# Two transformer blocks on one core: the attention pipeline's slots in another order, and one stream of groups in the second block

## The chip, the cores and the metric

The kernel runs on one core of a Trainium2 chip. The time is what the device needs for one execution of the whole program, in microseconds (us). All weights and activations are float32, and every matrix product goes through TensorE (PE), which also does the transposes. VectorE (DVE), ScalarE (ACT) and GpSimd (POOL) work beside it, each on its own list of instructions, strictly in order; semaphores tie the lists together.

## The reference

The reference runs two model blocks, one after the other, on 512 tokens of width 1024; each block has two layers, so there are four layers. A layer is an adaptive norm, a mixer of several kinds of attention, an output projection, and a feed-forward part. The change is in the attention of all four layers.

First block, per layer: a sparse attention (4 heads, top 128 keys chosen by an index score), a stick-breaking attention (4 heads) and a sliding-window attention with sinks (8 heads); their outputs are normed per head and projected:

```python
o = jnp.concatenate([oa, ob, oc], axis=2)
o = _rms(o, g_out).reshape(B, L, MIX_WIDTH)
return o @ w_o
```

Second block, per layer: a differential attention (4 heads, each with two score matrices), a latent attention (4 heads) and a state-space scan (8 heads):

```python
p = _masked_softmax(s1, mask) - lam * _masked_softmax(s2, mask)     # differential
o = jnp.einsum('bhqk,bkhe->bqhe', p.astype(v.dtype), v)
...
o = _rmsnorm(o, subln_g, SUBLN_EPS) * (1.0 - lambda_init)
...
p = _masked_softmax(sc, _chunk_mask(start, s))                      # latent
return jnp.einsum('bhqk,bkhe->bqhe', p.astype(v.dtype), v)
...
return jnp.concatenate([y_a, y_b, y_c], axis=-1) @ w_out
```

## The kernel before

**Order.** One list of steps per layer (`STEPS1`, `STEPS2`, built by `order1` and `order2`) is walked by every engine. Each engine picks out the steps in which it has a part and emits its instructions in that order; nothing is reordered afterwards. `woven` merges streams of steps: each stream gets a start and an end as fractions, its chunks are spread evenly between them, and the merged list is sorted by position.

**Groups.** Attention is cut into groups: some heads of one block of 128 queries. The first block has 8 window groups ("c", 4 heads each) and 6 sparse groups ("a"); the second has 6 latent groups ("m", numbers 0 to 5: 4 heads against 128 and 256 keys, then 2 heads against 384 and 512) and 12 differential groups ("d", numbers 6 to 17: 2 heads at a time for the first two query blocks, then one head at a time against 384 and 512 keys).

**Steps of a group** and who does them:

- `sc`: PE computes scores (L1339 in the first block, L1498 latent, L1509 differential); DVE adds the mask and takes the maximum while copying to SBUF (L2368; L2550, L2561); ACT takes the exponent (L1756; L1932).
- `cb` (only "d"): DVE joins the two exponents (L2581 to L2585).
- `tp`: PE transposes the weights (L1352; L1526), ACT copies them out of PSUM (L1767; L1942).
- `pv`: PE multiplies by the values (L1366; L1540), ACT copies the output and squares it (L1776, L1778; L1951, L1956), DVE sums the squares (L2387 to L2391; L2597 to L2602; for "m" a reciprocal, L2594).
- `on`: ACT takes logarithm and exponent, which make the root (L1784, L1786; L1963, L1965), DVE scales the output (L2149 to L2151 and L2400; L2614).
- `ot`: PE transposes the output (L1373; L1548), ACT copies it (L1794; L1973, L1975).

The rows of weights and the transposed weights have two buffers each. Slot j of `group_slots` and `group_slots2` holds steps of several groups: before, `on` of group j-3, `cb` of j-1, `sc` of j, then `pv` of j-2, `tp` of j-1, `ot` of j-3.

**What is woven between.** PE has other products that need none of this: projections of later tiles (`pj`, `proj`: L1264 and L1440; one chunk is two products of 128x512, each recorded as two instructions) and the first half of the output projection (`wo 0 n`: L1094, four such products for each of 8 steps). In the second block, before the change, the last four projection tiles (14 to 17, 16 chunks) run with the "m" groups, and a second stream weaves the 8 `wo 0` steps with the "d" groups. The steps `sz`, `sn 0`, `sn 1` norm the scan's output; `sn 1` must be done before `wo 0 0`. After the groups comes the second half of the output projection (`wo 1`), which needs every group's output. In the first block DVE also walks the rounds of the top-k (`topk`, L2303 and L2304) between the window groups.

## Time and profile before

| | us |
|---|---|
| median of 3 runs | 3133.03 |
| lowest, highest | 3124.57, 3137.35 |
| the profiled execution, its own time | 3130.37 |
| its span in the trace | 3128.6 |
| PE busy in that span | 2908.3 (93%) |
| DVE, ACT, POOL busy | 1787.2, 756.2, 931.1 |
| mean granted TensorE clock | 0.951 of full speed |

PE's busy time counts a matmul from its start to its modelled end, at whatever clock was granted; a stretch at half clock is busy too. The four attention stages take about 175 to 385, 955 to 1160, 1760 to 1894 and 2525 to 2659 us of the span; the feed-forward parts between them keep PE busy without a gap.

### The profile page before, as it was taken

The page shows a single profiled execution, that of the slowest core. Times are in us where ns is not written, and L with a number is a line of the kernel's source. Part 1 is how long each engine was busy: PE and PEld are TensorE (multiplying, and loading weights), DVE is VectorE, ACT ScalarE, POOL GpSimd, SP SyncE. Part 2 cuts the span into 40 slices and gives each one's busy share as a digit, 9 for nine tenths or more (in the row PEclk, how much of TensorE's full clock was granted, in tenths as well). Part 3 has the DMA queues.
Part 4 walks back from the last instruction along what each step waited for, and adds up shares of the span by engine and source line. Part 5 has one row for each costly group of instructions (what it writes and reads, how often), then busy time and mean ns, then how long its engine had stood idle before and what let it go on. Part 6 is the DMA issues. An engine that isn't in the chain of part 4 may idle for free.

```text
span 3128.6 us, 33693 instructions
## 1 busy us (share of the span) xinstructions
PE 2908.3 (93%) x12126; PEld 2133.1 (68%) x12126; DVE 1787.2 (57%) x3803; ACT 756.2 (24%) x1781; POOL 931.1 (30%) x794
## 2 busy tenths in 40 slices
PE   8888999999997899999989988999999998899997
PEld 4354688888544578888854456888884454688886
DVE  2673469388367447938854545877824634551433
ACT  2354310000235431000022353201112335320111
POOL 0301224443330124444412202344440400344442
PEclk9989999999998799999989988999999998899998
DMA  6115034244221013434421101254421210122221
GB/s 256 64 61 215 28 138 166 101 148 170 91 80 61 1 55 121 175 108 156 154 76 56 61 27 68 108 183 186 156 100 57 59 50 23 40 94 96 81 81 54
DMA packets 45412, 313.28 MB, mean 100 GB/s; under 512 B 5424, under 2 KB 5552, under 8 KB 31040
## 3 DMA queue, kind: packets, MB, share of 16 engines
q1 hardware_dynamic: 42912, 306.88, 27.0%
q10 hardware_dynamic: 2304, 4.20, 0.6%
q8 instruction: 98, 1.61, 0.2%
q14 instruction: 66, 0.54, 0.1%
q0 software_dynamic: 32, 0.07, 0.0%
HBM read 298.53 MB, written 2.10 MB: 96 GB/s over the span
## 4 chain that ended last, share of the span: by engine, by line
PE 70%; DVE 18%; ACT 6%; issue 3%; DMA 1%; POOL 1%; DVEq 0%; SPq 0%; ACTq 0%; POOLq 0%
PE bank L1114 39%; PE bank L1094 9%; PE bank L1440 7%; PE bank L1168 3%; DVE nw L2067 3%; PE bank L1264 2%; DVE sel L2304 2%; DVE m L2303 1%; PE bank L1307 1%; DVE SPT L2368 1%; ACT SPT L1756 1%; PE bank L1294 1%; PE bank L1229 1%; PE bank L1567 1%; DMA sel<-in_mod_pieces 1%
## 5 line engine op out<-in xcount | busy, mean ns | idle before, releaser
L1000 POOL TENSOR_TENSOR SPT<-ring 128x512 f32<-128x512 f32 (+2 forms) x140 | 175.2, 1252 | 956.3 <-DMA ring<-in_slabs 493.0
L1114 PE MATMUL bank<-U,ring 128*128 128x256 f32 x1728 | 412.2, 384 | 10.8 <-DVE U L2101 10.5
L1114 PEld LDWEIGHTS bank<-U,ring 128*128 128x128 f32 x1728 | 332.8, 193 | 58.4 <-DVE U L2101 12.5
L2067 DVE SCALAR_TENSOR_TENSOR nw<-sel,c,nw 128x256 f32<-128x256 f32 x504 | 321.7, 638 | 31.2 <-DMA sel<-in_mod_pieces 13.5
L1114 PE MATMUL bank<-U,SPT 128*128 128x256 f32 x1296 | 312.5, 381 | 3.0 <-POOL SPT L1005 3.0
L1114 PEld LDWEIGHTS bank<-U,SPT 128*128 128x128 f32 x1296 | 247.4, 191 | 37.7 <-POOL SPT L1005 4.4
L1114 PE MATMUL bank<-hT,SPT 128*128 128x256 f32 x1088 | 257.1, 379 | 0.0
L1440 PE MATMUL bank<-hT,ring 128*128 128x512 f32 x544 | 249.7, 607 | 7.1 <-ACT hT L1873 7.1
L2127 DVE TENSOR_TENSOR rb<-bank,nw 128x256 f32<-128x256 f32 x108 | 45.5, 422 | 355.9 <-PE bank L1114 259.1
L1114 PE MATMUL bank<-hT,ring 128*128 128x256 f32 x1088 | 246.1, 379 | 0.0
L1114 PEld LDWEIGHTS bank<-hT,ring 128*128 128x128 f32 x1088 | 207.0, 190 | 28.0 <-DMA ring<-in_slabs 0.3
L1114 PEld LDWEIGHTS bank<-hT,SPT 128*128 128x128 f32 x1088 | 207.1, 190 | 27.7
L1264 PE MATMUL bank<-hT,ring 128*128 128x512 f32 x448 | 211.8, 619 | 4.7 <-ACT hT L1650 4.7
L1440 PEld LDWEIGHTS bank<-hT,ring 128*128 128x128 f32 x544 | 102.5, 194 | 129.2 <-issue 124.8
L1612 ACT ACTIVATE nw<-bank 128x256 f32<-128x256 f32 x108 | 40.3, 374 | 607.1 <-PE bank L1114 607.1
L1003 POOL TENSOR_TENSOR SPT<-SPT,ring 128x512 f32<-128x512 f32 (+2 forms) x140 | 186.5, 1332 | 0.0
L1094 PE MATMUL bank<-U,ring 128*128 128x512 f32 (+2 forms) x416 | 179.1, 571 | 5.3 <-ACT U L1893 5.3
L1002 POOL TENSOR_TENSOR ring<-ring 128x512 f32<-128x512 f32 (+2 forms) x140 | 176.0, 1257 | 11.0
L1005 POOL TENSOR_TENSOR SPT<-ring,SPT 128x512 f32<-128x512 f32 (+2 forms) x140 | 175.8, 1256 | 11.0
L1264 PEld LDWEIGHTS bank<-hT,ring 128*128 128x128 f32 x448 | 85.7, 199 | 107.9 <-issue 105.9
L1094 PEld LDWEIGHTS bank<-U,ring 128*128 128x128 f32 (+1 forms) x416 | 82.1, 205 | 80.0 <-issue 69.1
L1114 PE MATMUL bank<-VT,SPT 128*128 128x256 f32 x544 | 129.3, 381 | 3.8 <-POOL SPT L1005 3.8
(344 smaller groups left out, 4501.9 us busy)
## 6 DMA issues: line engine op xcount, KB each, us to landing
ring<-in_slabs SPq DMA_DIRECT2D x86, 2048.0 KB, 8.0
sel<-in_mod_pieces SPq DMA_DIRECT2D x144, 512.0 KB, 4.5
ring<-in_slabs SPq DMA_DIRECT2D x8, 1536.0 KB, 7.0
ring<-in_slabs SPq DMA_DIRECT2D x8, 1280.0 KB, 8.3
tab<-U SPq DMA_DIRECT2D x40, 128.0 KB, 2.0
U<-in_slabs SPq DMA_DIRECT2D x2, 2048.0 KB, 22.5
tmp<-nw ACTq DMA_DIRECT2D x16, 256.0 KB, 2.9
ring<-in_slabs SPq DMA_DIRECT2D x2, 1808.0 KB, 11.7
```

The source lines that it names most:

```text
L1000: pool.tensor_tensor(e1, a21, a22, ALU.add).then_inc(*pool_order.up())
L1002: pool.tensor_tensor(a21, a11, a21, ALU.subtract).then_inc(*pool_order.up())
L1003: pool.tensor_tensor(e2, e1, a11, ALU.subtract).then_inc(*pool_order.up())
L1005: pool.tensor_tensor(e4, a12, e2, ALU.subtract).then_inc(*s["sx"].up())
L1094: mm = pe.matmul(dst, lhs(k), rhs(k), start=(k == 0), stop=(k == n - 1))
L1114: mm = pe.matmul(into[j][:, c:c + HALF], lhs[:, k, :], rhs[:, k, :], start=(begin and k == 0), stop=(end and k == kp - 1))
L1168: mm = pe.matmul(bank[b][:, c:c + HALF], lhs[:, k, :], rhs[:, k, :], start=(k == 0), stop=(k == KT // 2 - 1))
L1264: mm = pe.matmul(bank[b][:, :], w8[:, k, P * col:P * col + P], hT[:, k, :], start=(k == 0), stop=(k == KT - 1))
L1440: mm = pe.matmul(bank[b][:, :], w[:, k, c:c + P], hT[:, k, :], start=(k == 0), stop=(k == KT - 1))
L2067: ins = dve.scalar_tensor_tensor(a, w[:, k, :], c[:, j:j + 1], a, ALU.mult, ALU.add)
L2127: link(dve.tensor_tensor(sum2, b[1][:, 0:HALF], first[set_turn(bk, u)], ALU.add))
L2304: link(dve.match_replace(s, m8[:, :], s, TAKEN))
```

## The change

Both slot builders are written anew. A slot now has, in its first half, `ot` of group j-4, `pv` of j-2, a new step `ln` of j-3, and `sc` of j; in its second half `cb` and `tp` of j-1, a new step `rd` of j-2 and `on` of j-3. `ln` is ACT's part of the old `on`; `on` is left to DVE. `rd` is DVE's part of the old `pv`; `pv` is left to PE and ACT. There is one slot more per stream. In the second block the 16 chunks of tiles 14 to 17 are spread over the first third, the 8 `wo 0` steps over the rest, and all 18 groups run as one stream beside both. Two waits of DVE in `sc` are added, on its own earlier step.

```diff
@@ group_slots
-    for j in range(len(groups) + 3):
-        early, late = [], []
-        if 0 <= j - 3 < len(groups):
-            early.append(("on", groups[j - 3]))
-        if j < len(groups):
-            early.append(("sc", groups[j]))
-        if 0 <= j - 2 < len(groups):
-            late.append(("pv", groups[j - 2]))
-        if 0 <= j - 1 < len(groups):
-            late.append(("tp", groups[j - 1]))
-        if 0 <= j - 3 < len(groups):
-            late.append(("ot", groups[j - 3]))
+    for j in range(len(groups) + 4):
+        back = {d: groups[j - d] for d in range(5) if 0 <= j - d < len(groups)}
+        early = [(kind, back[d]) for kind, d in (("ot", 4), ("pv", 2), ("ln", 3), ("sc", 0)) if d in back]
+        late = [(kind, back[d]) for kind, d in (("rd", 2), ("on", 3), ("tp", 1)) if d in back]
@@ group_slots2
-        if 0 <= j - 1 < len(groups) and GROUPS2[groups[j - 1]][0] == "d":
-            early.append(("cb", groups[j - 1]))
...
+        early = [(kind, back[d]) for kind, d in (("ot", 4), ("pv", 2), ("ln", 3), ("sc", 0))
+                 if d in back and (kind != "ot" or back[d] in TURNS2)]
+        late = [(kind, back[d]) for kind, d in (("cb", 1), ("rd", 2), ("on", 3), ("tp", 1))
+                if d in back and (kind != "cb" or GROUPS2[back[d]][0] == "d")]
@@ order2
-    o += woven((0.01, 1, keys), (-0.15, 0.53, [[("sz",)], [("sn", 0)], [("sn", 1)]]),
-               (0.1, 1, [c for slot in slots[:NM2] for c in slot]))
-    o += woven((0.25, 1, [[("wo", 0, n)] for n in range(KT)]), (-0.15, 1.07, [c for slot in slots[NM2:] for c in slot]))
+    o += woven((-0.02, 0.33, keys), (-0.06, 0.24, [[("sz",)], [("sn", 0)], [("sn", 1)]]),
+               (0.33, 1.01, [[("wo", 0, n)] for n in range(KT)]), (0.04, 1.04, [c for slot in slots for c in slot]))
@@ ScalarE, both blocks
-                    elif kind == "on":
+                    elif kind == "ln":
@@ VectorE, both blocks
+                        if g >= 4:
+                            dve.wait_ge(*s1["un"].after(l, g - 3))
-                    elif kind == "pv":
+                    elif kind == "rd":
```

On DVE, among the "d" groups of the second block that see 512 keys. SPT and sel are the two rows of scores, cz the statistics; L2561 masks the scores, L2581 to L2585 join the two exponents of the group before, L2614 scales the output of an earlier group. Before:

```order
L2602 SCALAR_TENSOR_TENSOR cz<-cz 128x1
L2614 TENSOR_TENSOR SPT<-SPT,cz 128x64
L2581 RECIPROCAL cz<-cz 128x1
L2582 SCALAR_TENSOR_TENSOR cz<-cz,sm 128x1
L2585 SCALAR_TENSOR_TENSOR SPT<-sel,cz,SPT 128x384
L2561 ISA SPT,cz<-bank,cst 128x512
L2561 ISA cz 128x1
L2561 ISA sel,cz<-bank,cst 128x512
L2561 ISA cz 128x1
L2573 TENSOR_SCALAR cz<-cz 128x2
```

and in the changed kernel (L2548 masks, L2568 to L2572 join, L2584 to L2589 sum the squares, L2601 scales):

```order
L2548 ISA SPT,cz<-bank,cst 128x512
L2548 ISA cz 128x1
L2548 ISA sel,cz<-bank,cst 128x512
L2548 ISA cz 128x1
L2560 TENSOR_SCALAR cz<-cz 128x2
L2568 RECIPROCAL cz<-cz 128x1
L2569 SCALAR_TENSOR_TENSOR cz<-cz,sm 128x1
L2572 SCALAR_TENSOR_TENSOR SPT<-sel,cz,SPT 128x384
L2584 SCALAR_TENSOR_TENSOR cz<-cz 128x1
L2587 TENSOR_REDUCE cz<-SPT 128x1
L2589 SCALAR_TENSOR_TENSOR cz<-cz 128x1
L2601 TENSOR_TENSOR SPT<-SPT,cz 128x64
```

The join of the group before stood ahead of the mask and now stands behind it; the scaling stood ahead of the join and is now last.

On PE at the same place: L1509 scores, L1540 values, L1526 transposes of weights, L1548 transposes of outputs, L1094 the output projection. Before:

```order
L1509 MATMUL bank<-U 128x512 x2
L1540 MATMUL bank<-VT,yB 128x64 x3
L1526 MATMUL bank<-cst,SPT 128x128 x4
L1094 MATMUL bank<-U,ring 128x512 x4
L1509 MATMUL bank<-U 128x512 x2
L1540 MATMUL bank<-VT,yB 128x64 x4
L1526 MATMUL bank<-cst,SPT 128x128 x4
L1548 MATMUL bank<-cst,SPT 128x128
L1509 MATMUL bank<-U 128x512 x2
L1094 MATMUL bank<-U,ring 128x512 x4
```

and in the changed kernel (L1492 scores, L1523 values, L1509 transposes of weights, L1531 of outputs, L1077 the output projection):

```order
L1492 MATMUL bank<-U 128x512 x2
L1509 MATMUL bank<-cst,SPT 128x128 x3
L1077 MATMUL bank<-U,ring 128x512 x4
L1531 MATMUL bank<-cst,SPT 128x128
L1523 MATMUL bank<-VT,yB 128x64 x3
L1492 MATMUL bank<-U 128x512 x2
L1509 MATMUL bank<-cst,SPT 128x128 x4
L1523 MATMUL bank<-VT,yB 128x64 x4
L1492 MATMUL bank<-U 128x512 x2
```

The values of a group stood behind the scores of the group two later; now they stand ahead of those scores and behind the transposes of their own group.

On PE among the window groups of the first block: L1339 scores, L1264 projection chunks, L1366 values, L1352 and L1373 transposes. Before:

```order
L1339 MATMUL bank<-U 128x256 x4
L1264 MATMUL bank<-hT,ring 128x512 x2
L1366 MATMUL bank<-VT,yB 128x64 x8
L1352 MATMUL bank<-cst,SPT 128x128 x8
L1373 MATMUL bank<-cst,SPT 128x128 x2
L1264 MATMUL bank<-hT,ring 128x512 x4
```

and in the changed kernel (L1322 scores, L1247 projection chunks, L1335 and L1356 transposes, L1349 values):

```order
L1322 MATMUL bank<-U 128x256 x4
L1247 MATMUL bank<-hT,ring 128x512 x2
L1335 MATMUL bank<-cst,SPT 128x128 x8
L1247 MATMUL bank<-hT,ring 128x512 x2
L1356 MATMUL bank<-cst,SPT 128x128 x2
L1349 MATMUL bank<-VT,yB 128x64 x8
```

Here too the values now follow the transposes of their own group, with one projection chunk between them.

## Rows read from the trace of the kernel before

**Rows 1.** The page's chain that ended last, by engine, share of span.

```profile
PE 70%; DVE 18%; ACT 6%; issue 3%; DMA 1%; POOL 1%; DVEq 0%; SPq 0%; ACTq 0%; POOLq 0%
```

**Rows 2.** Windows: stretch, its length, busy PE, PEld, DVE, ACT, POOL, granted clock, DMA.

```profile
1759.98:1893.94 133.96, 119.58 (x489) 69.32 (x489) 52.00 (x223) 64.72 (x210) 0.00 (x0) 0.91 0.11 39
1819.60:1844.42 24.82, 20.19 (x62) 11.83 (x62) 12.36 (x57) 12.40 (x49) 0.00 (x0) 0.53 0.00 0
...
2524.70:2658.76 134.06, 119.32 (x489) 69.18 (x489) 52.00 (x222) 64.71 (x210) 0.00 (x0) 0.91 0.11 39
```

**Rows 3.** Waits of PE from 1760 to 1894: total us, times, longest.

```profile
PE bank L1526 <- DVE SPT L2585: 4.9, 7, 1.3
PE bank L1540 <- ACT yB L1942: 3.8, 4, 1.8
...
PE bank L1454 <- ACT sqb L1835: 1.7, 1, 1.7
```

**Rows 4.** Timeline of DVE, one "d" slot: start, duration, line, operation, count, wait.

```profile
1873.63 0.69 DVE L2561 CUSTOM_DVE_ANT_0 SPT<-bank,cst 128x512 f32<-128x512 f32 x1
...
1875.12 0.15 DVE L2597 SCALAR_TENSOR_TENSOR cz<-cz 128x1 f32<-128x1 f32 x1
...
1878.40 0.16 DVE L2581 RECIPROCAL cz<-cz 128x1 f32<-128x1 f32 x1
...
1879.52 0.68 DVE L2561 CUSTOM_DVE_ANT_0 SPT<-bank,cst 128x512 f32<-128x512 f32 x1
```

**Rows 5.** Timeline of ACT in the same slot.

```profile
1875.25 0.72 ACT L1932 ACTIVATE SPT<-SPT,cz 128x512 f32<-128x512 f32 x1 [2.90 <-DVE cz L2573]
...
1876.67 0.20 ACT L1951 ACTIVATE SPT<-bank 128x64 f32<-128x64 f32 x1
...
1877.07 0.58 ACT L1942 ACTIVATE yB<-bank 128x512 f32<-128x512 f32 x1
```

**Rows 6.** Timeline of PE over the "d" groups of the second block's first layer.

```profile
1812.13 0.71 PE L1509 MATMUL bank<-U 32*128 32x128 f32 x8 [0.78 <-ACT U L1882]
...
1838.85 5.74 PE L1094 MATMUL bank<-U,ring 128*128 128x512 f32 x8
...
1867.79 3.60 PE L1094 MATMUL bank<-U,ring 128*128 128x512 f32 x8
1871.32 1.13 PE L1509 MATMUL bank<-U 32*128 32x512 f32 x4
1872.37 1.10 PE L1540 MATMUL bank<-VT,yB 128*128 128x64 f32 x8
1873.86 0.63 PE L1526 MATMUL bank<-cst,SPT 128*128 128x128 f32 x4 [0.38 <-DVE SPT L2585]
...
1893.94 1.82 PE L1094 MATMUL bank<-hT,ring 128*128 128x256 f32 x4 [0.65 <-ACT hT L1975]
```

**Rows 7.** Windows around the fall of the clock in that layer.

```profile
1813.73:1817.82 4.09, 3.35 (x33) 3.02 (x33) 2.04 (x14) 2.94 (x12) 0.00 (x0) 1.00 0.98 417
1817.82:1821.92 4.10, 4.10 (x25) 2.94 (x24) 1.98 (x14) 2.24 (x11) 0.00 (x0) 0.65 0.05 16
```

**Rows 8.** Timeline of PE over window groups, first block, second layer.

```profile
981.11 1.13 PE L1339 MATMUL bank<-U 64*128 64x256 f32 x8
...
988.20 1.14 PE L1339 MATMUL bank<-U 64*128 64x256 f32 x8
...
1018.35 0.66 PE L1373 MATMUL bank<-cst,SPT 128*128 128x128 f32 x2 [3.30 <-DVE SPT L2400]
```

**Rows 9.** Timeline of DVE there: the first of a window group's four masks.

```profile
1001.36 0.42 DVE L2368 CUSTOM_DVE_ANT_0 SPT<-bank,cst 128x256 f32<-128x256 f32 x1
```

**Rows 10.** Timeline of ACT there: the first exponent, and the copies of transposed weights.

```profile
1003.32 0.51 ACT L1756 ACTIVATE SPT<-SPT,vec 128x256 f32<-128x256 f32 x1 [3.22 <-DVE vec L2377]
...
1005.39 0.36 ACT L1776 ACTIVATE SPT<-bank 128x256 f32<-128x256 f32 x1
...
1006.11 1.07 ACT L1767 ACTIVATE yB<-bank 128x512 f32<-128x512 f32 x2
```

More of the change, by code:

```diff
@@ L506, in group_slots2 @@
     out = []
-    for j in range(len(groups) + 3):
-        early, late = [], []
-        if 0 <= j - 3 < len(groups):
-            early.append(("on", groups[j - 3]))
-        if 0 <= j - 1 < len(groups) and GROUPS2[groups[j - 1]][0] == "d":
-            early.append(("cb", groups[j - 1]))
-        if j < len(groups):
-            early.append(("sc", groups[j]))
-        if 0 <= j - 2 < len(groups):
-            late.append(("pv", groups[j - 2]))
-        if 0 <= j - 1 < len(groups):
-            late.append(("tp", groups[j - 1]))
-        if 0 <= j - 3 < len(groups) and groups[j - 3] in TURNS2:
-            late.append(("ot", groups[j - 3]))
+    for j in range(len(groups) + 4):
+        back = {d: groups[j - d] for d in range(5) if 0 <= j - d < len(groups)}
+        early = [(kind, back[d]) for kind, d in (("ot", 4), ("pv", 2), ("ln", 3), ("sc", 0))
+                 if d in back and (kind != "ot" or back[d] in TURNS2)]
+        late = [(kind, back[d]) for kind, d in (("cb", 1), ("rd", 2), ("on", 3), ("tp", 1))
+                if d in back and (kind != "cb" or GROUPS2[back[d]][0] == "d")]
         out.append([early, late])
@@ L1957, in _ @@
                                            ACT.Square).then_inc(*s2["uq"].up())
-                    elif kind == "on" and GROUPS2[st[1]][0] == "d":
+                    elif kind == "ln" and GROUPS2[st[1]][0] == "d":
                         g = st[1]
@@ L2539, in _ @@
                         stat = statD[:, g % 4, :]
+                        if g >= 4:
+                            dve.wait_ge(*s2["un"].after(l, g - 3))
                         if g >= 2:
@@ L2587, in _ @@
                         ins.then_inc(*s2["pr"].up())
-                    elif kind == "pv":
+                    elif kind == "rd":
                         g = st[1]
```

## The prediction, made before the changed kernel was timed

> **What bounds the kernel now.** I read the chain that ended last first. It runs through PE for 70% of the span and through DVE for 18% [rows 1]; the reader should see that time is gained or lost where PE waits or runs at the low clock. Next the windows by stage. The change touches only attention, so I took one stage of the second block whole, from the first chunk of tile 14 to the first `wo 1` product: 133.96 us, with PE busy 119.58, so 14.4 idle, and a mean clock of 0.91 [rows 2]. The other layer has 134.06 with the same counts [rows 2], so whatever I find is paid twice. Inside the stage the clock was at its lower level (1.2 GHz) for about 25 us, from 1819.60 to 1844.42, with PE busy 20.19 of them [rows 2]. At full clock that work takes a little more than half, so the low clock costs some 9 us a layer. The price at the foot of the stage: 14.4 idle plus 9 of clock, 23 us a layer, is all that any order could win here.
>
> Then the waits: PE's transposes wait for DVE's join (4.9 us in 7 waits), its values wait for ACT's copy of the transposed weights (3.8 in 4), and the sums of `sn 0` wait for ACT's squares (1.7) [rows 3]. Last, one "d" slot on DVE and ACT. DVE masks from 1873.63 to 1875.12, then stands until the squares and the root have come, scales, joins from 1878.40 and masks the next at 1879.52 [rows 4]. The period is 5.9 us, and it is a ring: mask, exponent (1875.25 to 1876.67), square, sum, root, scale, join [rows 4, 5]. PE stands outside that ring: it has a projection step in most slots (1867.79, 3.6 us) and waits only 0.38 in the slot of 1871.32 [rows 6].
>
> **The change, part by part.**
>
> The ring of DVE and ACT goes. Root and sum move one slot back, so DVE no longer stands for them. That removes the reason for most of the 4.9 us of join waits. What is late next decides, and I read it from the new order.
>
> A new ring, through PE. In a "d" slot PE now has: values of j-2, scores of j, transposes of j-1, and then at once the values of j-1. DVE has the mask of j ahead of the join of j-1. So the transposes of j-1, which before needed only things long done, now wait for scores of j, mask of j and join of j-1; and the values of j-1 wait for ACT's copy, which nothing covers unless a projection step stands there. Length for one head and 512 keys, from the start of the scores: the first half of them is done at 0.56 (half of 1.13 [rows 6]), and DVE starts at 0.72 (each hop between engines is taken as 0.10 to 0.16, an estimate: the exponent starts 0.13 after DVE's row at 1875.12 [rows 4, 5]); the mask takes 1.49 (1873.63 to 1875.12) and the join 1.12 (1878.40 to 1879.52) with 0.08 for its last write [rows 4], so 3.41; hop to PE 0.14, transposes 0.63 [rows 6], hop 0.10, copy 0.58 [rows 5], hop 0.14, values 0.95 (1.10 less its overlap) [rows 6]. Sum 5.95 us. PE works 2.6 of them. A projection step (3.44 to 3.53: 1867.79 to 1871.32 [rows 6]) between transposes and values covers only the copy, and the slot is 8.1 to 8.5; between scores and transposes it covers mask and join, and the slot is 7.0. Of the eight steps, only `wo 0 0` and `wo 0 5` stand there. The exponent (1.42 [rows 5]) runs beside the join and is not late.
>
> The same sum for every slot, with shorter operations scaled by their columns (an estimate; slots of 384 keys 5.0, two-head slots of 256 keys 5.8): 6.2, 5.4, 7.9, 5.8, 7.9, 5.0, 7.6, 5.0, 8.1, 5.95, 7.0 for the slots of groups 6 to 16, and 16.1 from the scores of group 17 to `wo 1` (two projection steps in it). Together 88.0 us. Before, from the scores of group 6 at 1812.13 to 1893.94 [rows 6], it is 81.8, of which 1.8 (twice the 0.95 above, for twice the products) are values of group 4, which now come earlier: 80.0. So **+8 us a layer**, though the 80.0 hold 9 us of low clock and the 88.0 none. Bounds: if DVE and ACT ran a slot ahead after all, PE would need its work only, 62 us at full clock, -18; if each hop were 0.1 longer, +13.
>
> The "m" groups. Two projection chunks of 1.7 stand in every slot, and by the same durations a slot needs about 6.1 us of them and its own work against a ring of 5.2 (no join in it), so the ring is covered. `sn 0` comes later, which removes its wait of 1.7 [rows 3]; the values of group 0 now wait about that long for ACT. Zero, bounds -2 and +2.
>
> The clock. At 1817.82 to 1821.92 the mean clock was 0.65, so it fell inside, after a stretch with PE busy 3.35 of 4.09 in short products and no projection [rows 7]; the first projection step after it took 5.74 instead of 3.5, and the clock was back behind it [rows 6]. In the new "d" part nearly every second slot has no projection and PE busy for 2.6 of 5 to 6 us, less than in the stretch before that fall. The gaps between projection steps are 5 to 10 us. I take five steps that start at the low clock, 2.3 us each (5.74 less 3.44), and nothing for the short products but 0.5: **+12 us a layer**. Bounds: 0, and 36 if all of the part but the projections' ends ran at the low level (11 slots by 2, 6 steps by 2.3).
>
> The Trainium skill has two rules that bear on this. Page "TensorE: Matmul & The Clock Gate", section "HAM oscillation — how this bites in real kernels", lets the clock fall only over long idle gaps; by it the term would be 0, and the change +20 in all. The same page, section "A second HAM failure mode: psum-queue depth-cycling", has short idles between groups of matmuls making it swing; that is the term above. The fall of 1819 came with no wait of PE above 0.8 us near it, so this trace sides with the second.
>
> First block. Among the window groups PE ran without a wait at 7.09 us a slot (981.11 to 988.20 [rows 8]). The new ring there: scores until DVE can start 0.95, four masks and the maximum 1.96 (1001.36 to 1003.32), exponents 2.07 (1003.32 to 1005.39) and copies 1.07 (the row at 1006.11) [rows 9, 10]; the output copy and square that stood between them have moved ahead; then a hop 0.14, values 1.75: 7.95. Over five full slots **+4 us a layer**. The end of that stage doesn't gain: PE waited 3.30 for the last scaling [rows 8], and DVE still has the rest of the top-k in front of it. Bounds -2 and +7. In the stick-breaking part the slots are long and filled; the copy of transposed weights there no longer stands behind an exponent that waits for POOL. I take **-2 a layer**, bounds -6 and +4.
>
> Sum: 2 x (8 + 0 + 12 + 4 - 2) = +44. 3130.37 + 44 = 3174; the profiled execution lay 2.7 under the median of the runs, so **3177 us**. No term is in weights or transfers: the DMA share in the stage is 0.11 [rows 2].
>
> **The rivals.**
>
> *The clock stays up.* The new part has many short idles and none of PE's waits is over 2.5 us, so the granted clock may hold; then the term of 12 goes: 3133 + 20 = 3153. Against it is the fall at 1819 with smaller idles [rows 7]; this is also what the first of the two rules gives.
>
> *The ring doesn't close and the change is faster.* The ring needs that PE reach the transposes before DVE is through. If hops are short and the two waits overlap with projection steps more than I count, PE is bound by its own work: half of the 23 us a layer comes back, and 5 a layer of the drains in the first block. 3133 - 2 x 12 - 2 x 5 = 3099. It decides from the point at which a slot without projection takes under 4.3 us (5.95 less a share of the 3.3 us of idle). For it: PE's waits are named in the rows, and their causes are removed. Against: the order puts mask ahead of join on DVE, which no overlap can change.
>
> *Gain and loss cancel.* The new ring costs 8 a layer, but the one hole between the "m" and "d" streams is closed and the clock is held up there by `wo 0 0`, and the first block gains 10 a layer from its drains and from its own low-clock stretches: 3125 to 3149, middle 3136. The new steps then do nothing that can be measured.
>
> **How the numbers follow.** The forecast has 0.54 (3157 to 3215), the steady clock 0.14, cancelling 0.16, faster 0.16. 0.5% is 15.7 us, about what a measurement here can tell from no change, so "same" is 3117 to 3149. Slower takes the first two, 0.68; same 0.16; faster 0.16. The range 3118 to 3212 leaves out the faster case and the top of the first, nearly 2 in 10.
>
> **What would show it.** Right: in the profile after, PE's transposes of weights in the "d" slots wait for DVE's join some 2 us in slots without projection, ten or more times a layer, and its values wait for ACT's copy; slots of 512 keys take about 6.0 and 8.3 us; the stage takes 150 us or more instead of 134, with a mean clock under 0.91; the window slots of the first block take about 8 us, with waits for ACT's copy. Wrong: a stage under 134 us, or transposes that don't wait; then the ring was misread. A stage of 142 at a clock near 1.0 is the first rival.

## The result, and the profile of the changed kernel

The changed kernel takes 3236.25 us (median of 4 runs, 3230.43 to 3237.90) against 3133.92 us for the kernel before (4 runs, 3124.57 to 3137.35). The ratio is 1.0328, 95% interval 1.0302 to 1.0354: 3.3% slower. The forecast was 3177 with a range of 3118 to 3212, so the sign was right and the size was not: the loss is 102 us where 44 were expected.

The chain that ended last, by engine, has hardly moved (compare [rows 1]); it tells that PE's time still counts, not why there is more of it:

```profile
PE 72%; DVE 17%; ACT 4%; issue 3%; DMA 2%; POOL 1%; SPq 0%; DVEq 0%; ACTq 0%; POOLq 0%
```

The windows by stage do tell (columns as in [rows 2]). The first two rows of each kernel are the second block's first layer: the latent ("m") part, from its first scores to the scores of group 6, and the differential ("d") part, from there to the first `wo 1` product. The last row is the first block's window groups in its second layer. Changed kernel:

```profile
1788.78:1841.78 53.00, 49.73 (x194) 28.91 (x192) 12.61 (x49) 22.78 (x62) 0.00 (x0) 0.94 0.05 17
1841.78:1961.83 120.05, 84.11 (x285) 46.89 (x284) 36.71 (x169) 42.96 (x147) 0.00 (x0) 0.73 0.05 17
...
945.11:1042.15 97.04, 69.39 (x318) 43.45 (x318) 72.09 (x233) 41.42 (x142) 10.65 (x8) 0.86 0.14 52
```

Kernel before:

```profile
1763.96:1812.13 48.17, 45.74 (x182) 26.54 (x181) 12.90 (x50) 22.81 (x62) 0.00 (x0) 1.00 0.06 26
1812.13:1893.94 81.81, 69.87 (x299) 41.00 (x300) 36.60 (x168) 41.53 (x147) 0.00 (x0) 0.85 0.11 37
...
930.06:1018.94 88.88, 66.27 (x318) 40.83 (x318) 72.21 (x233) 40.20 (x142) 10.65 (x8) 0.87 0.16 57
```

The d part has grown by 38.2 us (and by 37.8 in the other layer), the m part by 4.8 (3.1), the window groups by 8.2 (8.1). Over whole layers the two traces differ by 15.0, 11.2, 40.3 and 41.0 us, 107.5 in all, which is the difference of the spans (3236.1 and 3128.6). DVE, ACT and POOL have the same busy time in each stage as before: no engine got more work, PE only waits and runs slower. One shift has to be kept in mind when the parts are compared: the values of group 4 (1.8 us, from 1839.95 to 1841.78) stood behind the scores of group 6 and now stand ahead of them, so they have moved from the d part into the m part. Like for like, the d part has grown by about 40 us and the m part by 3.0 and 1.3.

What PE waits for in the whole changed kernel (total us, times, longest):

```profile
PE bank L1509 <- DVE SPT L2572: 52.2, 18, 3.4
PE bank L1356 <- DVE SPT L2385: 24.7, 15, 3.5
...
PE bank L1523 <- ACT yB L1925: 19.6, 20, 1.9
```

These are the transposes of weights waiting for the join (10.1 us in 14 before), the first block's output transposes waiting for the scaling (10.3 in 6), and the values waiting for ACT's copy (7.6 in 8). All of the first row is in the two d parts (25.9 and 26.3 us, 9 waits each). Three slots of one, as PE saw them (start, duration, line, operation, count, wait; L1492 scores, L1509 transposes of weights, L1523 values, L1077 projection, L1531 output transposes):

```profile
1888.12 0.91 PE L1492 MATMUL bank<-U 32*128 32x384 f32 x4
1891.64 0.52 PE L1509 MATMUL bank<-cst,SPT 128*128 128x128 f32 x3 [2.61 <-DVE SPT L2572]
1892.89 1.51 PE L1523 MATMUL bank<-VT,yB 128*128 128x64 f32 x6 [0.73 <-ACT yB L1925]
1894.33 1.65 PE L1492 MATMUL bank<-U 32*128 32x384 f32 x4
1898.59 0.87 PE L1509 MATMUL bank<-cst,SPT 128*128 128x128 f32 x3 [2.61 <-DVE SPT L2572]
1899.25 5.32 PE L1077 MATMUL bank<-U,ring 128*128 128x512 f32 x8
1904.41 0.38 PE L1531 MATMUL bank<-cst,SPT 128*128 128x128 f32 x2
1904.63 0.78 PE L1523 MATMUL bank<-VT,yB 128*128 128x64 f32 x6
1905.34 0.92 PE L1492 MATMUL bank<-U 32*128 32x384 f32 x4
```

The scores at 1888.12 took 0.91, those at 1894.33 took 1.65 for the same four products, and those at 1905.34 took 0.92 again. The windows name the reason. The mean granted clock was 0.96, then 0.50 (1.2 GHz), and it came back to 2.4 GHz inside the projection step, which took 5.32 instead of 3.6.

```profile
1888.12:1892.89 4.77, 1.43 (x9) 0.64 (x8) 2.83 (x12) 2.78 (x10) 0.00 (x0) 0.96 0.01 2
1892.89:1899.25 6.36, 3.75 (x13) 2.52 (x14) 2.77 (x12) 2.08 (x8) 0.00 (x0) 0.50 0.00 0
1899.25:1904.41 5.16, 5.16 (x9) 2.09 (x9) 0.00 (x0) 0.49 (x1) 0.00 (x0) 0.66 0.02 5
```

And DVE in the first of these slots: both masks, then the join at 1890.87, which the transposes at 1891.64 have waited for. DVE had stood idle for 8 us when the scores reached it:

```profile
1889.20 0.56 DVE L2548 CUSTOM_DVE_ANT_0 SPT<-bank,cst 128x384 f32<-128x384 f32 x1 [8.00 <-PE bank L1492]
...
1890.87 0.62 DVE L2572 SCALAR_TENSOR_TENSOR SPT<-sel,cz,SPT 128x384 f32<-128x384 f32 x1
```

### The profile page after: what moved, and what is told of

Same layout as the page of the kernel before. It is cut to its first block, busy times and chain, and to the rows that moved or that the text cites. A ratio compares the mean times of both kernels' runs of the same rounds, so it can differ in the third digit from the quotient of the medians.

```text
span 3236.1 us, 33707 instructions
## 1 busy us (share of the span) xinstructions
PE 2953.2 (91%) x12126; PEld 2151.9 (66%) x12126; DVE 1792.9 (55%) x3803; ACT 763.5 (24%) x1781; POOL 931.0 (29%) x794
## 3 DMA queue, kind: packets, MB, share of 16 engines
q1 hardware_dynamic: 42912, 306.88, 26.3%
## 4 chain that ended last, share of the span: by engine, by line
PE 72%; DVE 17%; ACT 4%; issue 3%; DMA 2%; POOL 1%; SPq 0%; DVEq 0%; ACTq 0%; POOLq 0%
PE bank L1097 36%; PE bank L1077 10%; PE bank L1423 7%; PE bank L1151 3%; DVE nw L2050 3%; PE bank L1247 2%; DMA ring<-in_slabs 2%; PE bank L1523 1%; PE bank L1349 1%; DVE sel L2287 1%; PE bank L1290 1%; DVE m L2286 1%; PE bank L1277 1%; PE bank L1492 1%; PE bank L1212 1%
## 5 line engine op out<-in xcount | busy, mean ns | idle before, releaser
L2050 DVE SCALAR_TENSOR_TENSOR nw<-sel,c,nw 128x256 f32<-128x256 f32 x504 | 328.5, 652 | 30.4 <-DMA sel<-in_mod_pieces 12.7
L1247 PE MATMUL bank<-hT,ring 128*128 128x512 f32 x448 | 211.4, 617 | 4.7 <-ACT hT L1633 4.7
L1077 PE MATMUL bank<-U,ring 128*128 128x512 f32 (+2 forms) x416 | 198.5, 621 | 5.7 <-ACT U L1876 5.3
L1247 PEld LDWEIGHTS bank<-hT,ring 128*128 128x128 f32 x448 | 85.4, 198 | 106.5 <-issue 105.1
L1077 PEld LDWEIGHTS bank<-U,ring 128*128 128x128 f32 (+1 forms) x416 | 89.7, 224 | 90.3 <-issue 79.3
```

The costliest lines, as they stand in the source:

```text
L1077: mm = pe.matmul(dst, lhs(k), rhs(k), start=(k == 0), stop=(k == n - 1))
L1247: mm = pe.matmul(bank[b][:, :], w8[:, k, P * col:P * col + P], hT[:, k, :], start=(k == 0), stop=(k == KT - 1))
L2050: ins = dve.scalar_tensor_tensor(a, w[:, k, :], c[:, j:j + 1], a, ALU.mult, ALU.add)
```

## The experiments

Every kernel was run beside the kernel before; ratios are to it. The median of the kernel before lay between 3132.79 and 3138.65 in these sessions, so a difference of two times from different sessions is good to some 5 us; the ratios don't carry this shift. "d part" is always the stretch from the scores of group 6 to the first `wo 1` product. Theory A was: the order of the slots sends PE through DVE and ACT and back (the ring of the prediction), it opens when either of its links is cut, and the low clock follows from PE's waits. Its rivals were that the even spread of the projection steps makes the clock fall (theory B), and that the clock costs little.

**Join ahead of the masks (e1).** In the second block's slots (the lists of kinds and of how many groups back; the filters behind them stay):

```diff
-early: ("ot", 4), ("pv", 2), ("ln", 3), ("sc", 0)     late: ("cb", 1), ("rd", 2), ("on", 3), ("tp", 1)
+early: ("cb", 1), ("ot", 4), ("pv", 2), ("ln", 3), ("sc", 0)     late: ("rd", 2), ("on", 3), ("tp", 1)
```

> The changed kernel with one edit: in the second block's slots the join of group j-1 stands ahead of the masks of group j again (for every engine's order). Theory A (the ring through PE, scores - mask - join - transposes - copy - values - scores, made the loss, and the low clock is its consequence, since PE works for less than half of it): the waits of the transposes for the join (52.2 us in 18) fall under 12 us; the ring that is left goes scores - mask - exponent - copy of transposed weights - values, about 5.4 us for 512 keys; the stretch from the scores of group 6 to the first wo 1 product goes from 120.05 to about 97 with a mean clock over 0.82 instead of 0.73; time 3185 to 3195. Theory B (the projection steps spread evenly over the stage make the clock fall, whatever PE waits for): the join waits go, but the clock stays at 0.73 to 0.76 and the stretch at 110 or more; time 3212 to 3225.

Measured: 3196.80 us, ratio 1.0196 (1.0176 to 1.0216), d parts 103.63 and 101.99 at a mean clock of 0.77. The join is no longer among PE's waits; in its place the values wait for ACT's copy:

```profile
PE bank L1523 <- ACT yB L1925: 45.6, 22, 4.1
```

The ring moved: the copy stands behind the exponent on ACT, and the scores behind the values on PE. 39 us came back. The time lies between the two forecasts, the d part is 5 us or more longer than theory A's 97, and the clock stayed low: one cut doesn't open the ring, as theory A had it, but leaves a shorter one.

**Values behind the scores (e2).** The other link alone:

```diff
-early: ("ot", 4), ("pv", 2), ("ln", 3), ("sc", 0)     late: ("cb", 1), ("rd", 2), ("on", 3), ("tp", 1)
+early: ("ot", 4), ("ln", 3), ("sc", 0)     late: ("pv", 2), ("cb", 1), ("rd", 2), ("on", 3), ("tp", 1)
```

> The changed kernel with one edit: in the second block's slots the values of group j-2 stand behind the scores of group j, as before the change; masks stay ahead of the join. Theory A: PE is still sent from the scores through mask and join to the transposes (the join waits stay, some 35 to 50 us in all), but scores no longer wait for the copy of transposed weights; slot 4.3 to 5.2 us for 512 keys; stretch 120.05 to about 98; time 3185 to 3200. Theory A2 (the order of mask and join alone is the loss, the place of the values is free): no gain, 3230 to 3240. Theory B (the even spread of projection steps and the clock): 3215 to 3230.

Measured: 3182.74 us, ratio 1.0153 (1.0133 to 1.0174); d parts 100.49 and 98.36 at 0.76 and 0.79, join waits 33.0 us in 18; the m part 46.5 instead of 53.0 and 51.3 (1.8 of this is group 4's values, which are back in the d part). The place of the values is not free (theory A2 falls): it gave back 53 us, 2 more than theory A's range allowed and more than the join did.

**The weave alone (e4).** The kernel before with only the one stream:

```diff
-    o += woven((0.01, 1, keys), (-0.15, 0.53, [[("sz",)], [("sn", 0)], [("sn", 1)]]),
-               (0.1, 1, [c for slot in slots[:NM2] for c in slot]))
-    o += woven((0.25, 1, [[("wo", 0, n)] for n in range(KT)]), (-0.15, 1.07, [c for slot in slots[NM2:] for c in slot]))
+    o += woven((-0.02, 0.33, keys), (-0.06, 0.24, [[("sz",)], [("sn", 0)], [("sn", 1)]]),
+               (0.33, 1.01, [[("wo", 0, n)] for n in range(KT)]), (0.04, 1.04, [c for slot in slots for c in slot]))
```

> The kernel before with one part of the change alone: the second block's one stream of latent and differential groups with the first half of the output projection spread from a third of the stage to its end; all slots in their old order. Theory A: the slots' order made the loss, the weave alone moves the time little: 3125 to 3145, with the stretch from the scores of group 6 to the first wo 1 product at 78 to 88 us. Theory B: the even spread makes the clock fall: the mean clock of the stretch under 0.8, and half or more of the loss appears: 3165 to 3190.

Measured: 3139.24 us, ratio 1.0020 (1.0007 to 1.0033); d part 86.19 at a clock of 0.86, m part 45.22, together 131.4 against 130.0. Theory B falls: the loss is in the slots.

**Both links cut (e13).** The edits of e1 and e2 at once; the late root, the one stream and the first block stay as changed.

```diff
+early: ("ot", 4), ("cb", 1), ("ln", 3), ("sc", 0)     late: ("pv", 2), ("rd", 2), ("on", 3), ("tp", 1)
```

> The changed kernel with both edits of the second block's slots at once: join of group j-1 ahead of the masks of group j, and values of group j-2 behind the scores of group j; the root stays a slot later and the first block stays changed. Each alone gave back 39 and 53 us. Theory A (one ring, open once either link is cut, and the low clock follows it): with both cut PE has no round trip left, the stretch from the scores of group 6 to the first wo 1 product is 80 to 92 us, and the time 3150 to 3168, of which some 24 are the first block's. Theory E (each edit cuts only its own wait, and the low clock of 0.76 stays as in both runs): 3172 to 3182.

Measured: 3152.79 us, ratio 1.0051 (1.0033 to 1.0068):

```profile
1786.46:1832.99 46.53, 44.26 (x178) 25.59 (x177) 12.58 (x49) 22.80 (x62) 0.00 (x0) 1.00 0.02 8
1832.99:1915.93 82.94, 70.38 (x300) 41.67 (x300) 36.45 (x169) 42.09 (x148) 0.00 (x0) 0.86 0.07 27
```

The d part is back at 82.9 (81.8 before) with the clock at 0.86 (0.85 before), and nothing of the clock was touched by hand. This is theory A's number (3150 to 3168) and not theory E's (3172 to 3182). These two swaps are the loss of the second block: 83.5 us, where its two layers had grown by 81.3 in the traces. Each cut alone left the other half of the path and a clock of 0.76 to 0.79; only both together brought the clock back to what it was.

**Work added (e3, e5, e14).** How much of the loss is clock? The changed kernel with products of 128x512 written to the bank that the next step overwrites, where PE would stand waiting for the join (only where no projection step stands there); 5 products in e3, 3 in e5:

```diff
+                            if bare(l, g):
+                                for _ in range(FILL):
+                                    pe.matmul(bank[bk2.bank(l, st + (0,))][:, 0:SEQ], ident,
+                                              cst[:, C_CHUNK:C_CHUNK + SEQ], start=True, stop=True)
                             pe.wait_ge(*s2["pr"].after(l, g - NM2 + 1))
```

> The changed kernel with work added and nothing taken away: where no projection step stands between the scores and the transposes of a d group, PE computes five products of 128x512 into the bank that the transposes overwrite, while it would wait for the join (2.6 to 3.3 us each in the trace after). If the low clock is the larger part of the loss (20 us or more a layer: eight projection steps at 4.9 to 6.3 us instead of 3.5 make 14.7, the short products the rest), the clock rises from 0.73 to over 0.9 in the stretch, which shrinks from 120.05 to about 100, and the kernel with more work is faster: 3190 to 3205. If the low clock costs little and the ring's length is set by DVE and ACT, the time stays: 3232 to 3245.

> As the filled kernel, with three products of 128x512 instead of five in the same places (in the run before they took 4.56 us for five, so about 2.7 us for three, which is the length of the wait for the join, 2.6 to 3.0). If the filled run's gain was the clock's (27 us a layer) less 1.8 us of overshoot in each of 10 slots, then with the overshoot gone the stretch from the scores of group 6 to the first wo 1 product is 93 to 97 us at a clock over 0.9, and the time 3180 to 3192. If instead the fillers only took the place of waits and the clock term is 8 us a layer as the five-product run shows at first sight, the stretch is 108 to 113 and the time 3215 to 3225.

Measured: e3 3221.95 us (ratio 1.0283, 1.0258 to 1.0307), d parts 111.70 and 113.38 at 0.97 and 0.95. With five products, 4.56 us, PE overshoots a wait of 2.6 to 3.0 in every such slot, and the kernel is still 14 us faster than without them; the time lies between its two forecasts. e5, without the overshoot: 3197.93 us (1.0202, 1.0183 to 1.0222), d parts 103.25 at 0.92 and 98.81 at 0.97; more than the expected 93 to 97 (and the time above the expected 3192), with the clock low in the first slots. e14 adds one such product (two in the first slots) ahead of the values as well:

> The changed kernel with the three products of 128x512 before the bare transposes as in the run with three, and one more (two in the first two slots) ahead of the values of every d group, where PE waits 0.7 to 2 us for ACT's copy. In the run with three the clock was still low in the first two slots (a projection step of 6.1 us among them) and gave 98.8 and 103.3 us for the stretch. If the order's own length at full clock is 93 us, as the slots of the filled runs add up, the stretch is 93 to 98 in both layers at a clock of 0.97 or more, and the time 3185 to 3195. If the added products cost what the clock gives, it stays at 3195 to 3205.

Measured: 3190.90 us (1.0171, 1.0149 to 1.0192), within the forecast, d parts 98.99 and 99.33, 1 us above it, clock 1.00 in both. That is 45 us less than the changed kernel with 84 products more. One view now prices the clock, since both kernels run the same instructions in that part: PE's lines over the d part (busy, mean ns | idle before). Changed kernel:

```profile
L1077 PE MATMUL bank<-U,ring 128*128 128x512 f32 x64 | 42.7, 830 | 0.0
L1523 PE MATMUL bank<-VT,yB 128*128 128x64 f32 x97 | 17.4, 334 | 8.1 <-ACT yB L1925 8.1
L1492 PE MATMUL bank<-U 32*128 32x128 f32 (+3 forms) x64 | 15.7, 598 | 0.0
L1509 PE MATMUL bank<-cst,SPT 128*128 128x128 f32 x48 | 10.5, 353 | 25.9 <-DVE SPT L2572 25.9
```

The same at full clock (e14; its lines are shifted by the edit, and its added products, 25.6 and 15.1 us, are left out):

```profile
L1089 PE MATMUL bank<-U,ring 128*128 128x512 f32 x64 | 29.1, 597 | 0.0
...
L1542 PE MATMUL bank<-VT,yB 128*128 128x64 f32 x97 | 13.0, 273 | 0.2 <-ACT yB L1944 0.2
L1504 PE MATMUL bank<-U 32*128 32x128 f32 (+3 forms) x64 | 11.9, 467 | 0.0
L1525 PE MATMUL bank<-cst,SPT 128*128 128x128 f32 x48 | 7.8, 281 | 0.9 <-DVE SPT L2591 0.6
```

13.6 + 4.4 + 3.8 + 2.7 = 24.5 us a layer are the low clock, if all of it counts in PE's time (an estimate). The order itself is then 120.05 - 24.5 = 95.5 us long; from the other side, e14's 99.0 less the added products that stand where PE did not wait (four of 0.9 behind projection steps, 1.2 in the second slot) gives 94.2. What needs no such sum is the difference of the stretches, 120.05 - 98.99 = 21.1 us a layer: the clock costs at least that.

**The first block (e6, e11).** e6 moves only the output transposes of the window groups, from the slot's head to behind the scores; e11 puts the first block's slots back as before.

```diff
 (e6)
-early: ("ot", 4), ("pv", 2), ("ln", 3), ("sc", 0)
+early: ("pv", 2), ("ln", 3), ("sc", 0), ("ot", 4)
```

> The changed kernel with one edit in the first block's slots alone: the output transposes of group j-4 stand behind the scores of group j instead of at the slot's head. Theory C (in the first block the new loss of 8 us a layer comes from those transposes, which stand at PE's head and wait for DVE's scaling, 24.7 us in 15 waits, itself behind the masks): a window slot goes from 7.95 to 7.1, the waits for the scaling fall under 12 us, the time by 10 to 16: 3220 to 3226. Theory D (the ring of the prediction, scores - mask - exponent - copy - values - scores, is as long, 7.95 by its sum): the wait turns up at the values, for ACT's copy, and the slot stays at 7.7 to 8.0; time 3230 to 3237.

> The changed kernel with the first block's slots put back exactly as before the change, the second block untouched. By the stages of the two traces the first block holds 24 of the 107 us (8.1 in the window groups of each layer, 8.4 in the stick-breaking part of the first layer, -0.6 in that of the second) and one layer's feed-forward 3.8: theory A gives 3208 to 3215. If these 24 us are mostly chance in when the clock falls, it gives 3222 to 3234.

In the changed kernel a window slot (second layer) reads as below: output transposes (L1356) wait at PE's head for the scaling, which DVE does behind the masks. From scores to scores (L1322) it is 7.92, where it was 7.09 [rows 8].

```profile
1002.85 1.13 PE L1322 MATMUL bank<-U 64*128 64x256 f32 x8
...
1009.59 0.41 PE L1356 MATMUL bank<-cst,SPT 128*128 128x128 f32 x2 [1.54 <-DVE SPT L2385]
1009.84 1.00 PE L1349 MATMUL bank<-VT,yB 128*128 128x64 f32 x8
1010.77 1.13 PE L1322 MATMUL bank<-U 64*128 64x256 f32 x8
```

In e6 the same slot:

```profile
1001.93 1.13 PE L1322 MATMUL bank<-U 64*128 64x256 f32 x8
...
1008.49 1.08 PE L1349 MATMUL bank<-VT,yB 128*128 128x64 f32 x8 [1.19 <-ACT yB L1750]
1009.50 1.13 PE L1322 MATMUL bank<-U 64*128 64x256 f32 x8
```

7.57 us, and the wait is now ACT's copy; the slot behind it is 8.95 (1009.50 to 1018.45), as it was (8.88), and the window groups take 96.8 and 96.7 us instead of 97.1 and 97.0. Time 3229.06 (1.0304, 1.0287 to 1.0320). Slot and time both lie just outside theory D's ranges (7.7 to 8.0, 3230 to 3237) and farther from theory C's (7.1, 3220 to 3226), and the wait turned up where D had it: there are two rings of nearly one length, and opening one shows the other. The 7 us of the time don't come from the window groups; 3.4 of them are the m parts, whose order is the same in both kernels. e11: 3213.48 (1.0249, 1.0229 to 1.0269), 22.8 us back, within theory A's 3208 to 3215. Its window groups take 88.9 and 89.1, which is 16 of the 22.8.

**A third order (e7, e8, e9, e10, e12).** With the rings known, an order without one: sums at the head, join ahead of the masks, scores ahead of the values, scaling behind the masks. In the second block:

```diff
+early: ("rd", 3), ("ot", 4), ("ln", 3), ("cb", 1), ("sc", 0)     late: ("pv", 2), ("on", 3), ("tp", 1)
```

e7 has it with the one stream and the first block's old order, e8 with the two old streams.

> First block in its old order, one stream in the second, and there a third order: sums and the output's transposes at the head, join ahead of the masks, scores ahead of the values, scaling behind the masks, roots a slot later. By theory A no engine's slot then holds a round trip: DVE has 3.6 us of work in a 512-key slot, the shortest ring left is mask - exponent - join, 4.3 us, and PE has 2.6 us or 6.1 with a projection step. The stretch from the scores of group 6 to the first wo 1 product is 72 to 80 us against 81.8 before, the join waits under 5 us in all: 3105 to 3130, so a gain of up to 0.9% on the kernel before. If the low clock comes anyway, as it did before the change, the stretch is 80 to 88: 3130 to 3145.

> As the run ahead of it, with the two streams of the kernel before (the latent groups with the projection chunks, then the differential groups with the first half of the output projection). Same work, so by theory A within 6 us of it, and a few us lower, since the one stream alone cost 5 us: 3100 to 3130.

Measured: e7 3134.28 (1.0005, 0.9992 to 1.0018), e8 3128.96 (0.9985, 0.9975 to 0.9996); d parts 79.2 and 79.3 in e7, 78.4 and 77.0 in e8. So e7's d parts are as short as theory A had them and its time isn't; e8 is just inside its forecast. In both, the first block had the old order, but `range(len(groups) + 4)` still made one more, empty, slot, and the second block's latent part began 14.5 and 14.9 us later than before (1778.48 and 1778.84 against 1763.96). e9 differs from e8 by that one number:

```diff
-    for j in range(len(groups) + 4):
+    for j in range(len(groups) + 3):
```

> The kernel before with the second block's slots alone in the third order (root a slot later, join ahead of masks, scores ahead of values), the two old streams, and the first block exactly as before the change. In the two kernels just run the first block's slots had the old order but one more (empty) slot at the end of the row, which moves every step of it against the projections it is woven with; there the first block took 14 us more than before up to the second layer. If that shift of the weave costs 5 us or more a layer, this run is 3112 to 3122; if those 14 us were chance of the run, it stays at 3126 to 3131 as the run before it.

Measured: 3115.47 us (6 runs, 3111.44 to 3119.66), ratio 0.9937 (0.9920 to 0.9955). This beats both kernels, by 18 and by 121 us. Against e8 only the empty slot is gone, so the empty slot cost 13.5 us; in the traces 12.7 us lie in the first layer's stick-breaking part. That it does so because the weave places steps by their share of the row's length is read from `woven`, not measured.

```profile
1758.56:1806.62 48.06, 45.73 (x182) 26.43 (x181) 12.32 (x49) 22.88 (x62) 0.00 (x0) 1.00 0.06 26
1806.62:1883.83 77.21, 70.11 (x299) 41.18 (x300) 36.15 (x169) 41.14 (x148) 0.00 (x0) 0.85 0.08 30
```

The d part of e9 is 4.6 us shorter than before (4.8 in the other layer), and the clock is low in it as it was: 0.85 over 77.2 us with two levels is about 23 us at the lower one. The two d parts hold 9.4 of the 18.9 us by which the two traces differ. The rest lies in code that e9's edit leaves as it was: the second block's m groups began at 1758.56 instead of 1763.96, though the first block's instructions are the same. Over the six kernels whose first block has exactly the old order (before, e4, e9 to e12) that point lies anywhere from 1758.56 to 1772.72. So a gain is measured for e9, but only about half of it can be put down to the third order.

e10 and e12 add one product ahead of the transposes of groups 5 to 10, or two ahead of those of groups 5 to 9:

```diff
+                        if 5 <= g <= 10:
+                            for _ in range(1):
+                                pe.matmul(bank[bk2.bank(l, st + (0,))][:, 0:SEQ], ident,
+                                          cst[:, C_CHUNK:C_CHUNK + SEQ], start=True, stop=True)
```

> As the run ahead of it, with one product of 128x512 (0.9 us) added ahead of the transposes of groups 5 to 10 in the second block, where the granted clock was at its lower level for some 30 us a layer though PE was busy for nearly all of it. If large products among the small ones keep the clock up, the added 5.4 us a layer bring back 8 to 14: 6 to 16 us faster than the run ahead of it. If the clock falls all the same, it is 4 to 11 us slower.

> As the filled kernel ahead, with two products (1.8 us) ahead of the transposes of groups 5 to 9. If one product is too little to hold the clock and two do, this is 2 to 8 us under the one with one; if one holds it already, the additional 4 us a layer show as 4 to 8 us more.

Measured: e10 3114.54 (0.9941, 0.9922 to 0.9960), e12 3120.66 (0.9958, 0.9942 to 0.9973): neither is told apart from e9 with certainty, so no gain from added work is measured here. e10 fits neither of its forecasts (6 to 16 us faster, 4 to 11 slower), e12 the second of its two. In e10 the two layers, the same code, came out differently:

```profile
1809.58:1890.47 80.89, 75.83 (x312) 43.82 (x312) 36.42 (x169) 41.65 (x148) 0.00 (x0) 0.85 0.09 29
...
2570.28:2644.93 74.65, 68.62 (x312) 39.82 (x312) 36.37 (x169) 41.45 (x148) 0.00 (x0) 0.95 0.09 31
```

With two products the clock was 0.96 in both layers (d parts 76.30 and 76.34), and the added work cost what it gave back.

## Why the prediction was right and wrong, step by step

**The ring through PE: right as a mechanism, short in length.** The transposes wait for the join and the values for ACT's copy, nine times each in a d part; "ten or more" waits of some 2 us were forecast, and it is nine of 2.6 to 3.4. e13 shows that this order is the cause of the second block's loss. Its length at full clock was put at 88.0 and is 94 to 95.5: the term of +8 a layer should have been +14 to +15.5.

The term that was too small is DVE's start. The sum let DVE begin its first mask at 0.72, when half of the scores are done. Here is a slot of one head and 512 keys without a projection step, in the changed kernel, with PE's scores, DVE's first mask and PE's transposes:

```profile
1922.72 1.13 PE L1492 MATMUL bank<-U 32*128 32x512 f32 x4
1924.02 0.69 DVE L2548 CUSTOM_DVE_ANT_0 SPT<-bank,cst 128x512 f32<-128x512 f32 x1 [7.01 <-PE bank L1492]
1926.86 1.09 PE L1509 MATMUL bank<-cst,SPT 128*128 128x128 f32 x4 [3.01 <-DVE SPT L2572]
```

DVE began 1.30 after the scores did and 0.17 after the (modelled) end of the last of them, though the program lets it go when the first half is there; why is open. From the scores to the transposes it is 4.14 where the sum has 3.55, and mask and join took what was forecast. At full clock such a slot takes 6.54 (1909.15 to 1915.69 in e5) where 5.95 was forecast. The other slots without a projection step are short in the same way: 5.52 for 5.0 with one head and 384 keys, where DVE began 1.08 after the scores (1888.12 and 1889.20), and 6.84 for 5.8 with two heads. Over the slots of a d part this makes most of the missing 6.2 to 7.5 us (an estimate). With a projection step between scores and transposes the forecast was met (7.04 in e3, 7.0 forecast): there DVE's late start is covered.

**The clock: the term that failed.** Five projection steps at the low clock and 0.5 for all short products were taken, 12 us a layer. In the trace seven of the eight steps started at it (4.9 to 6.3 us each), 13.6 us, and the short products lost 10.9 more, 24.5 together. That is twice the term, inside its bound of 36. The step that failed is the choice between the bounds: the price was taken from projection steps alone, though [rows 6] had both kinds in the low stretch. The d part was forecast at 80.0 + 8 + 12 = 100 us and is 120.05; 7.5 of the missing 20 are the ring, 12.5 the clock, and over two layers that is 40 of the 59 us by which the time was missed.

Of the two rules weighed there, from the page "TensorE: Matmul & The Clock Gate" of the Trainium skill, the section "HAM oscillation — how this bites in real kernels" ties the fall of the clock to long idle gaps. This case doesn't bear that out as the only condition: in the kernel before, the clock fell at about 1819 with no wait of PE above 0.8 us near it [rows 6, 7]. In the changed kernel it fell in slots whose waits were 2.6 to 3.4 us, which can't decide between the two. The section "A second HAM failure mode: psum-queue depth-cycling" of the same page of the Trainium skill has short idles between groups of matmuls swing the clock between its levels; the trace agrees in this, with 0.96, 0.50 and back within three steps and a mean of 0.73.

**The m groups: forecast 0, measured +3.0 and +1.3.** The bare windows differ by 4.8 and 3.1, but 1.8 of that is group 4's values, which the sum had taken out of the d part. So about 50.0 us was forecast and 53.0 and 51.3 measured. e1 has the same order there and took 49.6 in both layers with a clock of 1.00, so the order's own length was right. What was missed is the clock here too: the values of group 0 wait 1.68 us for ACT's copy (at 1802.93 in the changed kernel), as forecast, and behind that wait the scores and the next projection chunk ran at the low clock, which cost 3.4 us in one layer and 1.7 in the other. The first layer ended above the bound of +2, the second inside it.

**The window groups: forecast +4 a layer, measured +8.1.** The slot of 7.95 was met (7.92, 7.94), but by luck: what PE waits for there is a second ring that the sum had not seen, its output transposes behind the scaling. With that one opened (e6) the forecast ring shows, and it is 7.57. The sum counted five slots at 0.86; two have it. The slot with twice the values (16 records of the line instead of 8) takes 8.88, and the start of the stage, which the sum left at nothing, lost 4.5 and 5.9 (from the scores of group 1 to those of group 4: in the first layer 29.9 us before, 34.4 after, in the second 28.5 and 34.4).

**The stick-breaking part: forecast -2, measured +8.4 and -0.5** (from the end of the window groups to the first `wo 1` product). Part of this is not the order's: kernels with exactly the old order there took 131.4 to 131.5 us (before, e9, e10, e12) or 136.8 (e4, e11) for the same steps in the first layer, and the changed one 139.9. In the second layer those six lie between 113.1 and 117.5, and the changed one at 117.0, so no effect is seen there. What picks between the lengths was not found. One slot more, which the change also brings and which the prediction left out, gives 144.1 and 144.2 in the first layer where it is empty (e7, e8).

**The rivals.** The steady clock fell with the clock's 0.73 (its premise, no wait of PE over 2.5 us, fell too), the open ring with the first row of waits. "Gain and loss cancel" was right in one half: the hole between the two streams did close, and e4 shows that this is worth nothing.

**Open.** The first layer's feed-forward block took within 1 us of the same time and the second's 3.8 us more than before, in code that the change does not touch; kernels with the same code there differ by as much. The second of these is not quite without gaps: PE was busy for 380.90 of its 396.38 us in the changed kernel. What makes the clock fall where PE is busy was not found. Which of e1's and e2's links costs more cannot be said, since the two don't add: 39 and 53 us alone, 83.5 together.

## What to carry to other kernels

When a step's engines each work through a fixed list, follow one round trip: what must PE have issued before DVE can start, and what stands on DVE and ACT ahead of what PE needs next. Two harmless-looking swaps, masks ahead of join and values ahead of scores, closed a ring in which each of the three engines stood idle for the others; undone alone they gave 39 and 53 us of the 83.5. In such a sum, read from a row when the next engine starts, instead of letting it start at the first moment that the program allows. Where two kernels share code, compare that code too: here it moved by up to 14 us between kernels, as much as some of the effects. Price the low clock for every product in the stretch, not for the large ones alone, and treat a weave by shares as moved whenever its number of slots changes.

## What the hardware showed that was not expected

In the changed kernel the granted clock fell inside single slots, with PE waiting no more than 3.4 us at a time, and came back within one projection step (0.96, 0.50, then 0.66 on the way back, in the windows shown); it did so about every second slot. In each d part 27 added products (e5) or 42 (e14) brought the mean clock from 0.73 to 0.92 and 0.97, or to 1.00, and a kernel with more work ran 38 to 45 us faster. Where PE hardly waited (e9, against e10 and e12) the same means gave nothing that could be measured, and the same code could get a clock of 0.85 in one layer and 0.95 in the next.
